# Group norm, bonus and gate of a recurrent mixer moved into its scan, and the output projection into the same block

## The reference

```python
y = wkv7_scan(r_h, decay, k_h, v_h, -kk, kk * a_h)
mean = jnp.mean(y, -1, keepdims=True)                 # per token and head
var = jnp.mean(jnp.square(y - mean), -1, keepdims=True)
y = ((y - mean) * lax.rsqrt(var + GN_EPS)).reshape(B, S, D)
y = y * ln_w + ln_b
bonus = jnp.sum(r_h * k_h * r_k, -1, keepdims=True) * v_h
y = y + bonus.reshape(B, S, D)
return (y * g) @ w_o                                  # g = sigmoid(xg @ g1) @ g2
```

## Time and profile before

| | us |
|---|---|
| median of 3 runs | 3177.93 (3176.54 to 3177.95) |
| the profiled execution | 3176.2 |
| its span in the trace | 3174.3 |
| TensorE busy with matmuls, over the span | 2879.1 (91%) |
| VectorE busy | 1582.4 (50%) |
| ScalarE busy | 999.6 (31%) |
| GpSimd busy | 668.2 (21%) |
| mean granted TensorE clock | 0.938 of 2.4 GHz |

### The profile page before, as it was taken

One profiled execution on the slowest core, in us unless ns is written; L12 is line 12 of the kernel. 1 busy time (PEld: TensorE's weight loads), 2 busy tenths in 40 slices (PEclk: granted clock), 3 DMA queues, 4 the chain that ended last, 5 costly groups with the idle time before them and its releaser, 6 DMA issues. The chain is left out here.

```text
span 3174.3 us, 38092 instructions
## 1 busy us (share of the span) xinstructions
PE 2879.1 (91%) x13928; PEld 2287.0 (72%) x13928; DVE 1582.4 (50%) x1976; ACT 999.6 (31%) x1522; POOL 668.2 (21%) x632
## 2 busy tenths in 40 slices
PE   6799999799899699999699786689999888999999
PEld 4678888457799568888488673368888664688887
DVE  3377763645544567763425374545343427663432
ACT  3324332234312233332233342332222234732221
POOL 0021111331800222112000060632111102431100
PEclk9899999899999699999899787899999998999999
DMA  3122323211100022223133000213233320032333
GB/s 129 67 67 93 99 89 99 80 47 60 41 1 1 9 69 97 97 89 97 58 99 94 26 1 1 47 56 104 93 99 89 90 80 1 8 100 93 99 89 104
DMA packets 79430, 218.80 MB, mean 69 GB/s; under 512 B 21806, under 2 KB 21934, under 8 KB 78799
## 3 DMA queue, kind: packets, MB, share of 16 engines
q1 hardware_dynamic: 78878, 213.29, 21.5%
q10 hardware_dynamic: 432, 3.90, 0.3%
HBM read 215.06 MB, written 2.10 MB: 68 GB/s over the span
## 5 line engine op out<-in xcount | busy, mean ns | idle before, releaser
L281 PE MATMUL psum<-rounded,high_r 128*128 128x512 f32 x3040 | 1200.6, 395 | 65.7 <-DVE rounded L246 41.4
L283 PE MATMUL psum<-rounded,high_r 128*128 128x512 f32 x3040 | 1190.2, 392 | 0.0
L285 PE MATMUL psum<-rounded,ring_low 128*128 128x512 f32 x3040 | 1189.4, 391 | 0.0
L301 ACT ACTIVATE high_r<-ring 128x1024 fp32r<-128x1024 f32 (+2 forms) x432 | 420.2, 973 | 1490.0 <-PE psum L285 1449.5
L306 DVE TENSOR_TENSOR ring_low<-ring,high_r 128x1024 fp32r<-128x1024 f32 (+2 forms) x432 | 519.9, 1204 | 701.2 <-ACT high_r L301 699.9
L281 PEld LDWEIGHTS psum<-rounded,high_r 128*128 128x128 f32 x3040 | 574.8, 189 | 208.8 <-issue 55.4
L285 PEld LDWEIGHTS psum<-rounded,ring_low 128*128 128x128 f32 x3040 | 575.2, 189 | 120.8
L283 PEld LDWEIGHTS psum<-rounded,high_r 128*128 128x128 f32 x3040 | 575.6, 189 | 120.1 <-issue 2.6
L658 DVE TENSOR_TENSOR arena<-psum,inverse 128x512 f32<-128x512 f32 x176 | 121.5, 691 | 314.0 <-PE psum L285 313.8
L558 POOL CAST rounded<-rows 128x512 f32 (+1 forms) x88 | 53.8, 611 | 784.8 <-DVE rows L663 784.8
L1721 POOL TENSOR_SCALAR arena<-arena,small 128x512 f32<-128x512 f32 x64 | 99.7, 1564 | 196.6 <-DVE small L1690 195.7
(11 more groups left out here) (309 smaller groups left out, 2967.6 us busy)
## 6 DMA issues: line engine op xcount, KB each, us to landing
ring<-in_up SPq DMA_DIRECT2D x176, 512.0 KB, 3.2
ring<-in_down SPq DMA_DIRECT2D x64, 384.0 KB, 3.1
ring<-in_down SPq DMA_DIRECT2D x64, 320.0 KB, 2.9
ring<-in_even_in SPq DMA_DIRECT2D x36, 512.0 KB, 3.6
ring<-in_sgu_in SPq DMA_DIRECT2D x16, 512.0 KB, 3.3
ring<-in_even_out SPq DMA_DIRECT2D x16, 384.0 KB, 3.1
ring<-in_qkv SPq DMA_DIRECT2D x12, 512.0 KB, 3.6
ring<-in_sgu_out SPq DMA_DIRECT2D x8, 512.0 KB, 3.2
```

The lines of the kernel that those rows point to most:

```text
L281: nc.tensor.matmul(psum[:, m, :], high_r[:, r % HIGHS, blk], x_high, start=(k0 + k == 0), stop=False)
L283: nc.tensor.matmul(psum[:, m, :], high_r[:, r % HIGHS, blk], x_low, start=False, stop=False)
L285: mm = nc.tensor.matmul(psum[:, m, :], ring_low[:, r % R, blk], x_high, start=False, stop=end)
L301: nc.scalar.activation(high_r[:, r % HIGHS, 0:nk * P], ring[:, r % R, 0:nk * P], ACT.Copy).then_inc(unit_high, 1)
```

## The change

The three phases behind the scan are gone, and `rwkv()` with its `feed_forward` stands in one block (`joined()`): the projection follows the scan without a meeting of the engines, and all 105 semaphores are cleared behind the feed-forward. The norm is worked out for five groups: heads 0 to 7 of all chunks (n = 0), then heads 8 to 15 of one chunk each (n = 1 to 4).

- **ScalarE.** `keep_y` makes four copies of 128x64 with the sum in an accumulator, one small scaling to minus the mean, and four squares of 128x64, with the sum in an accumulator again. In units 8 to 11 it also takes the bonus sums out. `root(n)` stands at the ends of units 9, 11, 13 and behind `keep_y(14)`. It also spreads the 32-row rest of the gate's hidden rows to four strips, and splits the first two projection weight units.
- **TensorE.** `bonus_sums` (eight matmuls of 32 output columns, each in the strip of 32 partitions of its tile, 256 tokens) ahead of `output(8)` and `output(9)`, two transposes ahead of `output(10)` and `output(11)`, four gate matmuls inside unit 15. Behind the scan: four strip matmuls, four tiles turned, four gate matmuls, four strip matmuls, four tiles turned.
- **GpSimd.** The eight products r k (from `y_done` 8 on), the norm of groups 0 to 3 and their bonus (`whiten`), the low halves of two weight units and of four input tiles.
- **VectorE.** `variance` and `invert` on small tiles in the scan, the norm of group 4, eight gate products, four low halves.
- **SyncE.** Two loads during the scan (`rwkv_post`, 768 KB: ln_w as rows, rest of g2, r_k by heads; `lora_g2`, 512 KB) in place of two behind it.

```diff
+        def joined():
+            with nc.Block() as block:
+                open_block.append(block)
+                yield
+                open_block.pop()
+            clear(to_clear)
...
+                    sp.wait_ge(y_done, 8)
+                    sp.wait_ge(spread_out, 8 * BLOCKS)
+                    sp.dma_start(work[:, 0:3, :], dram["rwkv_post"]).then_inc(post_loaded, 16)
+                    sp.dma_start(rows[:, 0:2, :], dram["lora_g2"]).then_inc(g2_loaded, 16)
...
+                    def bonus_sums(h):
+                        pe.wait_ge(paired, KD)
+                        pe.wait_ge(post_loaded, 16)
+                        for i in range(KD):
+                            q = i % 4
+                            nc.tensor.matmul(psum[q * 32:(q + 1) * 32, 7, HALF:2 * HALF], r_k_heads[:, i * 32:(i + 1) * 32],
+                                             read_key(i)[:, h * HALF:(h + 1) * HALF], start=(i < 4), stop=(i >= 4))
...
+                    def gate(n):
+                        if n >= 4:
+                            pe.wait_ge(g2_kept, n - 3)
+                        nc.tensor.matmul(psum[:, n % 4, :], g2[:, n * P:(n + 1) * P], hidden_g, start=True, stop=False)
...
+                    def turn_output(i):
+                        if i == 0:
+                            pe.wait_ge(applied, 1)
+                        if i == 3:
+                            pe.wait_ge(y_kept, UNITS)
+                        if i == 4:
+                            pe.wait_ge(applied, 4)
+                            pe.wait_ge(last_applied, 1)
+                        if i >= 4:
+                            pe.wait_ge(gated, i - 3)
...
                     output(UNITS - 1)
+                    gate_rest(0)
+                    for i in range(4):
+                        turn_output(i)
+                    for n in range(4, KD):
+                        gate(n)
+                    gate_rest(4)
+                    for i in range(4, KD):
+                        turn_output(i)
...
-                        nc.scalar.activation(yt[:, c, 2 * i0 * HD:(2 * i0 + 4) * HD], psum[:, 7, 0:4 * HD], ACT.Copy).then_inc(y_kept, 1)
+                        for j in range(4):
+                            nc.scalar.activation(yt[:, c, (2 * i0 + j) * HD:(2 * i0 + j + 1) * HD], psum[:, 7, j * HD:(j + 1) * HD],
+                                                 ACT.Copy, accum_out=mean[:, at + j:at + j + 1]).then_inc(y_summed, 1)
...
+                        act.wait_ge(y_summed, 4 * u + 4)
+                        nc.scalar.activation(mean[:, at:at + 4], mean[:, at:at + 4], ACT.Copy, scale=-1.0 / HD).then_inc(y_mean, 1)
+                        act.wait_ge(y_mean, u + 1)
+                        for j in range(4):
+                            x = psum[:, 7, j * HD:(j + 1) * HD]
+                            sq = nc.scalar.activation(x, x, ACT.Square, bias=mean[:, at + j:at + j + 1],
+                                                      accum_out=var[:, at + j:at + j + 1])
+                        sq.then_inc(y_kept, 1)
...
                     keep_y(UNITS - 1)
+                    for m in range(4):
+                        keep_gate(m)
+                    root(4)
+                    split_high(act, Stream("rwkv_o"), 0, 1)
+                    for i in range(4):
+                        output_high(i)
+                    for m in range(4, KD):
+                        keep_gate(m)
+                    for i in range(4, KD):
+                        output_high(i)
...
+                    variance(4, UNITS)
+                    invert(4)
+                    for n, (with_, op) in enumerate(((spread_over(mean, 4), ALU.add), (spread_over(var, 4), ALU.mult),
+                                                     (ln_w_of(4), ALU.mult), (v_of(4), ALU.add))):
...
+                    for i in range(KD):
+                        dve.wait_ge(y_turned, i + 1)
+                        dve.wait_ge(g2_kept, i + 1)
+                        nc.vector.scalar_tensor_tensor(out=tile(RR + i), in0=psum[:, 4 + i % 4, :], scalar=col("ln_b", i), in1=tile(KK + i),
+                                                       op0=ALU.add, op1=ALU.mult).then_inc(gated, 1)
+                        if i > 4:
+                            output_low(i - 1)
+                    output_low(KD - 1)
...
+                    whiten(0)
+                    whiten(1)
+                    whiten(2)
+                    weights_low(0)
+                    whiten(3)
+                    pool.wait_ge(y_done, UNITS)
+                    nc.gpsimd.tensor_tensor(v_of(4), v_of(4), spread_over(bonus, 4), ALU.mult).then_inc(last_bonus, 1)
+                    weights_low(1)
+                    for i in range(4):
+                        pool.wait_ge(o_high, i + 1)
+                        nc.gpsimd.tensor_tensor(rounded(RR)[:, i, :], tile(RR + i), rounded(XN)[:, i, :].bitcast(F32),
+                                                ALU.subtract).then_inc(o_low_first, 1)
```

More of the change, by code:

```diff
@@ L333, in body_of @@
                 return body
-            if name in SPLIT_LATE:
+            if name in SPLIT_LATE and name not in SPLIT_BEFORE:
                 split(eng, st, 0, 0)
@@ L757, in rwkv @@
             N, RB, AK, RK = range(4)
+            mean, var, bonus = small[:, 0:64], small[:, 128:192], roots[:, :]
+            ln_w_rows = flat(work[:, 0:2, :])
+            g2_rest, r_k_heads, bonus_rows = work[:, 2, 0:256], work[:, 2, 256:512], work[:, 3, :]
+            g2 = flat(rows[:, 0:2, :])
+            HALF = 2 * CH
             def whole_of(s):
@@ L1105, in output @@
                             pe.wait_ge(y_kept, u)
+                        if u in (8, 9):
+                            bonus_sums(u - 8)
+                        if u in (10, 11):
+                            turn_bonus(u - 10)
                         for j in range(4):
@@ L1140, in _ @@
                             score(u + 1, 1)
+                        else:
+                            gate(2)
                         round_of(u, 1)
+                        if not more:
+                            gate(3)
                         turn_keys(u)
@@ new lines, in _, with whiten @@
+                    pool.wait_ge(y_done, 8)
+                    for i in range(KD):
+                        nc.gpsimd.tensor_tensor(read_key(i), tile(RR + i), tile(KK + i), ALU.mult).then_inc(paired, 1)
+                    done = [0]
+                    def whiten(n):
+                        y, v = y_of(n), v_of(n)
+                        pool.wait_ge(y_inverted, n + 1)
+                        if n == 0:
+                            pool.wait_ge(post_loaded, 16)
+                        for to, with_, op in ((y, spread_over(mean, n), ALU.add), (y, spread_over(var, n), ALU.mult),
+                                              (y, ln_w_of(n), ALU.mult), (v, spread_over(bonus, n), ALU.mult)):
+                            if n == 0 and to is v:
+                                pool.wait_ge(y_kept, 12)
+                            wait(pool, normed_pool, done[0])
+                            nc.gpsimd.tensor_tensor(to, to, with_, op).then_inc(normed_pool, 1)
+                            done[0] += 1
+                        pool.wait_ge(normed_pool, done[0])
+                        nc.gpsimd.tensor_tensor(y, y, v, ALU.add).then_inc(applied, 1)
@@ L2248, in build @@
         sgu()
-        rwkv()
+        with joined():
+            rwkv()
         final_norm()
@@ L2271, in constants @@
             head_cols[2 * t + e, t, e * HD:(e + 1) * HD] = 1.0
-    halves = np.zeros((P, 2), np.float32)
-    halves[i, i // HD] = 1.0
     group_rows = np.zeros((P, 132), np.float32)
```

224 lines of the change are left out of this document (133 added, 91 removed).

## The result

The changed kernel takes 3123.23 us (median of 4 runs, 3121.67 to 3123.35) where the kernel before takes 3177.94: 54.7 us less, a ratio of 0.9825 with a 95% interval of 0.9808 to 0.9842. The forecast was 3129. The profiled execution took 3123.35 us, its span 3121.2.

A forecast was written before the change was run, and what follows sets the result against it. TensorE was taken to bound the scan, and behind it no engine, only steps in series. Scan +5.5 and 25.5 us behind T0 put the comparison point at 1083.5 against 1132.9: -49.4, so 3177.9 becomes 3129; range 3116 to 3143.

The forecast's parts named there:

- the point of comparison: End of the projection's first weight unit (unit 0), from which the old course takes over; forecast 1083.5 against old 1132.9.
- bonus_sums: TensorE in the scan: eight matmuls per call, pairs side by side, 2.1 us per call, 4.2 for both.
- The wait for GpSimd: In the scan, TensorE waits 1.1 us for GpSimd's eight products before the first bonus_sums call; between nothing and 3.5.
- Unit 15: Four gate matmuls laid into waits cost +2.7 us, the full clock gives back more: -0.9 together, ends +2.7 and -2.
- The port: In the scan, GpSimd's whiten and VectorE's two-input L1425 block each other; only whiten(1) should meet the pair: +0.5 us.
- the port rival: In the scan, whiten(0) drifts a unit later and meets L1425 six times: about 22 us, time 3150; chance 0.06.
- ScalarE: In the scan, keep_y grows to 4.1 us from 0.38, hidden by the idle 6.16 us before keep_keys: costs nothing.
- T0: The end of output(15), the scan's last output; forecast to move from 1052.5 to 1058.0.
- Step 1: First step behind the scan: keep_y(15) on ScalarE, 4.1 us from T0.
- step 2: Behind the scan on ScalarE: keep_gate 0 to 3 (4 x 0.60) and root(4) behind them (0.26), done at 6.8 us.
- Step 8: TensorE's slow start in the projection: 1.7 us lost, now falling into unit 1, bringing the path to 25.5.
- the first rival: Strips don't overlap (8.4 for 4.2) and the clock stays low behind T0, gates some 6 us later: 3139; chance 0.17.

The follow-up runs named there:

- one_strip: Changed kernel with all eight bonus_sums matmuls sent to the same 32 output partitions instead of four strips; 3125.75 us, +2.5.
- gates_behind: Changed kernel with the four gate matmuls of unit 15 moved behind output(15); 3129.05 us, +5.8.
- extra_3: Changed kernel with three extra, unread ScalarE copies of 128x512 ahead of the squares in keep_y of units 3 to 13; 3120.21 us, -3.0.
- the run with the guard: Changed kernel with GpSimd also waiting for the unit's four small state operations before whiten(0)'s bonus product; 3119.86 us, -3.4.

## Why the prediction was right, step by step

The total at the point of comparison was -49.4 and came out at -50.15, and the chain that it names behind the scan is the one in the trace. But that the total came so close is luck, a sum of errors that cancel: the scan cost 3.8 more than forecast and the tail gave 4.4 more.

**The scan** (+5.5 forecast, +9.3 measured). 7.2 of the 9.3 stand before the first changed unit and are longer drops of the clock, 4.9 of them the second one; one_strip's profile, without them, has the same code there. From unit 7 on it is +2.1, by units: +1.9 in unit 8 (strips 1.07, wait for GpSimd's products 1.19, and a clock that had been at 0.95 there), -1.6 in unit 9 (0.7 added, and the drop to 0.81 that the kernel before had there didn't come), +0.2 each in units 10 and 11, +3.65 in unit 12, -2.3 in unit 15.
- *bonus_sums*, 2.1 per call: 1.07. I took pairs side by side and held four at a time as an end of the range; the second end was right, and one_strip shows the price without it.
- *The wait for GpSimd*, 1.1: 1.19, with eight products in 9.86 us. *turn_bonus*, 0.6: 0.3.
- *Unit 15*, -0.9: -2.26, a little past its own lower end of -2, at the full clock as forecast; gates_behind shows the other side of it.
- *The port*, 0.5: 3.65. I had put whiten(0)'s last two operations "behind keep_y(11)" and left it there. Behind keep_y(11) means 2.7 us behind an output, and the earlier trace rows has an L1425 at 2.8. With the 4.1 us forecast for keep_y the product would have started behind that pair, and in extra_3, where it starts 4.5 us behind the output, unit 12 has no stall: it is the cheaper keep_y that brought the two together, by 0.10 us. It is one stall of the six of the port rival, whose sum is too high: six of (3.5 to 4.9, less 0.9) are 20 at most on average and 15 with the first of each pair halved, not 22, so that its time is 3143 rather than 3150. Its evidence is stronger than it says: the 5.45 of L1513 hold a wait too, since it starts 0.09 behind GpSimd's first product (1.26 us), so by this estimate L1523 lost 6.1 and not 4.95, and 6.1 is what L1531 still had to run when it started.
- *ScalarE*: hidden, as said, and cheaper than said, 2.4 to 2.6 us in place of 4.1. The reads of the accumulator take 202 ns each, as in the earlier trace rows, but start 0.1 us (copy) or 0.2 us (square) behind the start of their activation, and the next activation starts 0.1 behind them: a copy with its sum costs 0.20 from start to start, a square 0.29, where I had added durations (0.43, 0.52).

The groups by form on ACT, columns as in the earlier trace rows:

```profile
L1407 ACT ACTIVATION_READ_ACCUMULATOR psum<-psum,small 128x1 f32 x64 | 12.9, 202 | 0.0
L1392 ACT ACTIVATION_READ_ACCUMULATOR arena<-psum 128x1 f32 x64 | 12.8, 202 | 0.2
```

**The tail** (25.5 forecast, 21.07 measured), from T0, forecast and then measured: keep_y(15) 4.1, 2.4; root 6.8, 4.6; VectorE's four operations 12.4, 9.7; high(3) 15.9, 13.0; keep_gate 7 18.3, 15.0; VectorE's last low half 23.1, 20.0; end of the unit 23.8, 21.1. Step 1 was 1.7 too long and step 2 another 0.5; from there the differences are within 1 us, the block by GpSimd (2.4 forecast, 2.03 measured) among them. Step 8, the slow start of 1.7, didn't come: the clock was 0.92 over these 21 us. TensorE was busy for 17.82 of them, and the first rival's condition, a tail at half clock, wasn't met. The strips of gate_rest ran four side by side: 1.14 us for four matmuls of 512 columns, of which one alone takes 1.05.

**Behind it** (0 forecast, -3.0 measured). From SyncE's issue to the end of the span the kernel before takes 3174.3 - 1133.01 = 2041.3 us and the changed one 2038.3; the twelve others lie between 2037.8 and 2040.3. So the one profile of the kernel before lies outside the other thirteen, if only just, though no instruction there differs. The windows show where 2.3 of it is, at sums of squares by float32 matmuls (L458 before, L474 here) and what lies between, and what it is; of the kernel before, then of the changed one:

```profile
1930.48:1945.76 15.28, 9.83 (x16) 4.00 (x16) 4.43 (x2) 5.99 (x9) 0.00 (x0) 0.66 0.00 1
1945.76:1976.37 30.61, 20.34 (x32) 7.40 (x32) 15.01 (x19) 10.37 (x17) 0.00 (x0) 0.78 0.00 1
```

```profile
1880.24:1894.21 13.97, 8.53 (x16) 3.52 (x16) 4.43 (x2) 5.99 (x9) 0.00 (x0) 0.76 0.00 0
1894.21:1923.83 29.62, 19.60 (x32) 7.00 (x32) 15.01 (x18) 10.38 (x17) 0.00 (x0) 0.83 0.00 0
```

All other engines are busy for the same time; TensorE had more of the full clock (0.76 for 0.66, 0.83 for 0.78). Why the clock comes back earlier there, and why the first two drops of the scan last 7 and 10 us in one execution and 10 and 20 in another of the same code, stays open: I have no edit that moves it on purpose.

## What to carry to other kernels

An operation that another engine lets go is a stall waiting to happen if it can hold up the engine that is on the path (here GpSimd's 3.62 us before a VectorE operation of 0.29 with two SBUF inputs): look not at the unit it falls into but at the microsecond, and put a wait on the victim's semaphore in front of it; here that one wait was worth 3.4 us and the order of one root 4.0. An idle gap in front of an instruction is only a lower bound on its slack, and what hurts first can be another instruction (here the freeing of a PSUM bank, not keep_keys): lengthen it until it hurts, and read who waits for whom, before you call an engine full. Measure edits of one order together, since a copy that is free in idle time costs its whole length once the idle time is gone.

## What the runs showed of the hardware

- A small VectorE operation with one SBUF input is held up by GpSimd too: the variance (tensor_scalar, 128x8) took 2.86 us in place of 0.16 in the run with the guard, and ended 0.04 behind GpSimd's operation of 4.51. The Trainium skill (SBUF — State Buffer, Who interferes with whom) lists tensor_scalar among what can take the shared pair; I had only looked for two inputs.
- A wait of 2 us of TensorE was followed by half clock in one execution and not in another (unit 12, 0.89 and 1.00), and TensorE stayed at half clock for 10 or for 20 us while busy nearly throughout (20.62 of 21.00 us). The Trainium skill (TensorE: Matmul & The Clock Gate, HAM oscillation) describes a clock that falls after gaps in TensorE's work; the trace agrees where it falls (0.51 from 922 to 943 us, behind a wait of some 2 us) but not in unit 12 of one_strip, where it stayed at 1.00. This makes single profiles of this kernel differ by up to 7 us at the same instruction.
